# Two layers of a hybrid decoder on one core: a transpose moved to another PSUM bank and the layer norm's first steps issued ahead of the head norms

## The reference

```python
h = _rmsnorm(x, mix_norm_g[l])
a_b, a_c, a_x, s_u, s_v, q, k, v, gates = _split_cols(h @ w_in[l])
ya = _short_conv(a_b, a_c, a_x, conv_w[l], conv_b[l])
# spatial gating: v goes through gelu, a layer norm, then a causal 128x128 mixing
v = _layernorm(jax.nn.gelu(s_v), ln_g, ln_b);  yb = gelu(s_u) * (tril(w_s) @ v + b)
# stick-breaking attention, 8 heads x 64
qh = _rmsnorm(q.reshape(B, S, 8, 64), q_norm_g[l]); kh = _rmsnorm(k..., k_norm_g[l])
yc = _stick_breaking(qh, kh, vh)
x = x + (sum_i sigmoid(gate_i) * (y_i @ w_branch_out[i])) @ w_o[l]
x = x + SwiGLU(_rmsnorm(x, ffn_norm_g[l]))
```

## Time and profile before

| | us |
|---|---|
| three runs, median (lowest to highest) | 1691.32 (1690.37 to 1693.25) |
| profiled execution, its own time | 1691.32 |
| its span from first to last instruction | 1689.6 |
| PE busy / DVE / ACT / POOL | 1673.9 / 970.6 / 738.0 / 220.3 |

### The profile page before, as it was taken

The page is one execution under the profiler, slowest core; times in us unless marked ns, Lnnn a source line. Parts: engine busy times, 40 slices in busy tenths (PEclk is TensorE's granted clock), DMA queues, the critical chain, the costliest instruction groups (busy, mean ns, idle before and its releaser), DMA issues.

```text
span 1689.6 us, 22191 instructions
## 1 busy us (share of the span) xinstructions
PE 1673.9 (99%) x7651; PEld 1392.9 (82%) x7651; DVE 970.6 (57%) x1180; ACT 738.0 (44%) x1033; POOL 220.3 (13%) x204
## 2 busy tenths in 40 slices
PE   8999999999999999999999999999999999999998
PEld 6888888888888888888878888888888888888887
DVE  6887876554555434434659877765555543444344
ACT  5677676433343223223346776763333432232232
POOL 3343221000130000000323233200002100000000
PEclk9999999999999999999999999999999999999999
DMA  6232323333333333333333222223333333333333
GB/s 173 81 97 75 99 63 90 91 92 95 106 96 92 99 100 98 90 98 99 116 109 100 75 87 87 87 69 99 94 99 100 93 94 100 99 95 93 99 99 112
DMA packets 307416, 162.19 MB, mean 96 GB/s; under 512 B 5424, under 2 KB 303528, under 8 KB 307368
## 3 DMA queue, kind: packets, MB, share of 16 engines
q1 hardware_dynamic: 305064, 157.37, 31.9%
q10 hardware_dynamic: 2304, 4.20, 0.7%
HBM read 155.25 MB, written 2.10 MB: 93 GB/s over the span
## 4 chain that ended last, share of the span: by engine, by line
PE 92%; DVE 3%; DVEq 2%; ACT 1%; POOLq 0%; issue 0%; POOL 0%; DMA 0%; ACTq 0%; SPq 0%
PE bank L525 28%; PE bank L529 28%; PE bank L526 28%; PE z L598 2%; PE z L529 1%; PE z L525 1%; PE z L526 1%; DVEq L1594 1%; PE z L571 1%; PE misc L614 1%; PE misc L612 1%; PE z L572 1%; DVE S L1323 0%; DMA gates<-in_x 0%; DVE w_lo L1192 0%
## 5 line engine op out<-in xcount | busy, mean ns | idle before, releaser
L525 PE MATMUL bank<-xg_hi,w_hi 128*128 128x512 f32 x1584 | 622.7, 393 | 2.1 <-DVE xg_lo L1599 2.1
L526 PE MATMUL bank<-xg_lo,w_hi 128*128 128x512 f32 x1584 | 617.7, 390 | 0.0
L836 ACT ACTIVATE w_hi<-raw 128x1024 fp32r<-128x1024 f32 (+1 forms) x296 | 305.5, 1035 | 550.0 <-DMA raw<-in_w_gate_up 223.6
L1192 DVE TENSOR_TENSOR w_lo<-raw,w_hi 128x1024 fp32r<-128x1024 f32 (+1 forms) x296 | 387.2, 1311 | 37.6 <-ACT w_hi L836 21.3
L529 PE MATMUL bank<-xg_hi,w_lo 128*128 128x512 f32 x1584 | 392.4, 389 | 0.0
L525 PEld LDWEIGHTS bank<-xg_hi,w_hi 128*128 128x128 f32 x1584 | 298.0, 188 | 64.3 <-DVE xg_lo L1599 2.5
L526 PEld LDWEIGHTS bank<-xg_lo,w_hi 128*128 128x128 f32 x1584 | 298.1, 188 | 61.4 <-issue 0.7
L529 PEld LDWEIGHTS bank<-xg_hi,w_lo 128*128 128x128 f32 x1584 | 297.3, 188 | 62.1 <-issue 0.5
L1197 DVE TENSOR_TENSOR S<-bank,rstd 128x512 f32<-128x512 f32 x152 | 104.9, 690 | 267.5 <-PE bank L529 266.9
L525 PE MATMUL bank<-mid_hi,w_hi 128*128 128x512 f32 x480 | 186.9, 389 | 0.0
L526 PE MATMUL bank<-mid_lo,w_hi 128*128 128x512 f32 x480 | 186.7, 389 | 0.0
(11 more groups left out here) (205 smaller groups left out, 1689.9 us busy)
## 6 DMA issues: line engine op xcount, KB each, us to landing
raw<-in_w_in SPq DMA_DIRECT2D x112, 512.0 KB, 3.7
raw<-in_w_gate_up SPq DMA_DIRECT2D x88, 512.0 KB, 3.8
raw<-in_w_down SPq DMA_DIRECT2D x48, 512.0 KB, 3.5
raw<-in_w_branch_out SPq DMA_DIRECT2D x16, 512.0 KB, 3.6
raw<-in_w_o SPq DMA_DIRECT2D x16, 512.0 KB, 3.5
raw<-in_w_branch_out SPq DMA_DIRECT2D x16, 256.0 KB, 2.6
gates<-in_x SPq DMA_DIRECT2D x4, 512.0 KB, 7.1
mix_hi<-yb_hi ACTq DMA_DIRECT2D x8, 256.0 KB, 2.3
```

The source lines that it names most:

```text
L525: mm(dst[:, :], wh[:, k0 + k, :], his[k], start=(k % per == 0), stop=False)
L526: mm(dst[:, :], wh[:, k0 + k, :], los[k], start=False, stop=False)
L836: af(w_hi[at.slot(c)][:, 0:kc, :], raw[at.slot(c)][:, 0:kc, :], ACT.Copy).then_inc(hi_done, 1)
L1192: tt(w[:, 0:kc, :], r[:, 0:kc, :], h[:, 0:kc, :].bitcast(F32), ALU.subtract).then_inc(lo_done, 1)
```

## The change

The fourth `v` block's transpose goes to the bank `misc` instead of `z[0]`, and stands alone between units 5 and 6. The Q squares' two matmuls go from behind unit 5 to behind unit 6, the K squares' from behind unit 6 to behind unit 7. `misc` is thus lent five times in the stage instead of four (`M_P`), and POOL's K squares wait for one count more of `misc_done`. On ACT the fourth `keep_tokens` and the layer norm's four tiny operations now stand ahead of both `rms_chain`s, and the K rounding stands behind the first `ln_round`. On DVE the statistics stand right behind `scaled(5)`, the inverse root's last steps ahead of both `head_norm`s, `layer_norm(0)` ahead of `q_rest`, and `head_norm` of K ahead of `layer_norm(1)`. Seven small tiles get other addresses; none of them shares its place with another in either version.

```diff
-M_P, M_PAIR, M_PAIR_LAST = 4, 6, 3
+M_P, M_PAIR, M_PAIR_LAST = 5, 6, 3
@@ tiles: eps, par, gain0 now behind sw_lo, conv_in behind KT
-        sv_bank = [z[0], z[2], z[1], z[0]]
+        sv_bank = [z[0], z[2], z[1]]
@@ gpsimd
-                head_square(l * 8 + 2, KT, m0 + 2)
+                head_square(l * 8 + 2, KT, m0 + 3)
@@ tensor
                 unit(at, 5, xh, xl)
-                head_squares(m0 + 1, l * 8 + 1)
-                pe.wait_ge(sv_ok, l * 4 + 4)
-                pe.wait_ge(sv_kept, l * 4 + 1)
-                turn(sv_bank[3], lambda n: gates[:, 3, n * P:(n + 1) * P]).then_inc(sv_turned, 1)
+                four_transposes(m0 + 1, lambda n: gates[:, 3, n * P:(n + 1) * P], sv_ok, l * 4 + 4)
                 unit(at, 6, xh, xl)
-                head_squares(m0 + 2, l * 8 + 2)
+                head_squares(m0 + 2, l * 8 + 1)
                 unit(at, 7, xh, xl)
+                head_squares(m0 + 3, l * 8 + 2)
                 unit(at, 8, xh, xl)
-                four_transposes(m0 + 3, lambda n: sw_raw[:, n, :], sw_masked, l + 1)
+                four_transposes(m0 + 4, lambda n: sw_raw[:, n, :], sw_masked, l + 1)
@@ scalar
                 split_hi(at, 8)
+                act.wait_ge(misc_done, m0 + 2)
+                keep_tokens(3, misc).then_inc(sv_kept, 1)
+                act.drain()
+                act.sem_inc(misc_free, 1)
                 ln_exp_table()
-                act.wait_ge(misc_done, m0 + 2)
-                rms_chain(nchain + 1, misc, HD, misc_free)
-                act.wait_ge(sv_turned, l * 4 + 4)
-                keep_tokens(3, sv_bank[3]).then_inc(sv_kept, 1)
-                split_hi(at, 9)
-                act.wait_ge(qk_nrm, l * 8 + 1)
-                q_round()
-                act.wait_ge(misc_done, m0 + 3)
-                rms_chain(nchain + 2, misc, HD, misc_free)
                 act.wait_ge(ln_var, l + 1)
                 ... (the layer norm's four tiny operations)
-                split_hi(at, 10)
+                act.wait_ge(misc_done, m0 + 3)
+                rms_chain(nchain + 1, misc, HD, misc_free)
+                split_hi(at, 9)
+                act.wait_ge(qk_nrm, l * 8 + 1)
+                q_round()
+                act.wait_ge(misc_done, m0 + 4)
+                rms_chain(nchain + 2, misc, HD, misc_free)
+                ln_round(l, 0)
                 act.wait_ge(qk_nrm, l * 8 + 2)
                 k_round()
-                ln_round(l, 0)
+                split_hi(at, 10)
                 ln_round(l, 1)
+                ln_round(l, 2)
                 split_hi(at, 11)
-                ln_round(l, 2)
@@ vector
                 scaled(at, 5, KT[:, :])
-                split_lo(at, 8)
-                head_norm(nchain + 1, QT, par[:, R_GQ:R_GQ + 1])
                 ... (bn_stats and bn_aggr of the four token blocks)
+                split_lo(at, 8)
                 scaled(at, 6, gates[:, 4, :])
-                q_rest(l * 8 + 1)
-                split_lo(at, 9)
-                head_norm(nchain + 2, KT, par[:, R_GK:R_GK + 1])
-                scaled(at, 7, gates[:, 5, :])
                 ... (the inverse root's last steps, ln_t and ln_rstd)
+                head_norm(nchain + 1, QT, par[:, R_GQ:R_GQ + 1])
+                split_lo(at, 9)
                 layer_norm(0)
+                q_rest(l * 8 + 1)
+                scaled(at, 7, gates[:, 5, :])
+                head_norm(nchain + 2, KT, par[:, R_GK:R_GK + 1])
                 layer_norm(1)
+                layer_norm_lo(0)
                 split_lo(at, 10)
-                layer_norm_lo(0)
                 layer_norm(2)
```

More of the change, by code:

```diff
@@ L149, in build @@
         sw_lo = sb("sw_lo", [P, KC, P], F32R)
+        eps = sb("eps", [P, 1])
+        par = sb("par", [P, 64])
+        gain0 = sb("gain0", [P, KD])
         ya_hi = sb("ya_hi", [P, KC, T], F32R)
@@ L174, in build @@
         KT = sb("KT", [P, T])
+        conv_in = sb("conv_in", [P, 2 + T])
         N0 = sb("N0", [P, T])
         N1 = sb("N1", [P, T])
+        N2 = conv_in[:, 2:2 + T]
+        sq_sum, sq_one = S2[:, :], N1[:, :]
         over = plan[0]
@@ L199, in build @@
         plan[0] = max(plan[0], over + 16 * 4 * T)
[L200 to L205, removed]
         assert plan[0] <= nc.sbuf_usable_end, plan[0]
@@ L967, in _ @@
                 for c in range(3):
-                    act.wait_ge(sv_turned, l * 4 + c + 1)
+                    act.wait_ge(sv_turned, l * 3 + c + 1)
                     keep_tokens(c, sv_bank[c]).then_inc(sv_kept, 1)
                 split_hi(at, 8)
+                act.wait_ge(misc_done, m0 + 2)
+                keep_tokens(3, misc).then_inc(sv_kept, 1)
+                act.drain()
+                act.sem_inc(misc_free, 1)
                 ln_exp_table()
-                act.wait_ge(misc_done, m0 + 2)
-                rms_chain(nchain + 1, misc, HD, misc_free)
-                act.wait_ge(sv_turned, l * 4 + 4)
-                keep_tokens(3, sv_bank[3]).then_inc(sv_kept, 1)
-                split_hi(at, 9)
-                act.wait_ge(qk_nrm, l * 8 + 1)
-                q_round()
-                act.wait_ge(misc_done, m0 + 3)
-                rms_chain(nchain + 2, misc, HD, misc_free)
                 act.wait_ge(ln_var, l + 1)
@@ L989, in _ @@
                 af(ln_t[:, :], ln_r[:, :], ACT.Square).then_inc(ln_chain, 1)
-                split_hi(at, 10)
+                act.wait_ge(misc_done, m0 + 3)
[6 more added lines that the diff above has]
+                ln_round(l, 0)
                 act.wait_ge(qk_nrm, l * 8 + 2)
                 k_round()
-                ln_round(l, 0)
+                split_hi(at, 10)
                 ln_round(l, 1)
+                ln_round(l, 2)
                 split_hi(at, 11)
-                ln_round(l, 2)
-                act.wait_ge(misc_done, m0 + 4)
+                act.wait_ge(misc_done, m0 + 5)
                 af(sw_hi[:, :, :], misc[:, :].rearrange("p (g t) -> p g t", g=KC), ACT.Copy).then_inc(sw_hi_ok, 1)
```

## The result

| | before | after |
|---|---|---|
| median of 4 runs, us | 1691.7 (1690.37 to 1693.25) | 1707.45 (1707.22 to 1708.33) |
| ratio to before | | 1.0094, 95% interval 1.0082 to 1.0107 |
| profiled execution / its span | 1691.32 / 1689.6 | 1705.47 / 1703.8 |

The kernel became 15.8 us slower. The forecast was 1697.2, with a range to 1699.4: the direction was right, the forecast rise of 5.9 us a little over a third of what came.

A forecast was written before the change was run, and what follows sets the result against it. The prediction took PE's own work to bound the kernel: 1691.3 + 4.2 (net waits at the first scores, 2.1 in each of two layers) + 1.7 (one half-clock stretch) = 1697.2 us, range 1692.6 to 1699.4.

The forecast's parts named there:

- The moved tile addresses: Small tiles at new addresses: no instruction's shape changes, so cost 0, with no bound known but the measurement's.
- PE's own list: PE's matmuls and transposes in stage P: same number of each, only reordered, so its own work changes by 0.
- The K path: Q squares to K rest, stage P: K rest starts at 73.4, PE waits 2.3 us at the first scores, net 2.1 per layer.
- case A: The forecast itself: `layer_norm_lo(0)` goes ahead of POOL's K rest, wait 2.3 us a layer, 1695.5 to 1698.9 us; chance 0.62.
- the 0.4 at the next pair's squares: PE's 0.21 us wait for the next pair's K squares: 0.2 us comes back per layer.
- Same busy sums: Second layer's stage P is the first's shifted by 834.4 us, so the net 2.1 us counts twice: 4.2 us.
- The K squares: POOL's K squares in stage P: done by 61.8, needed at 63.46, margin 1.6 us; the last holds DVE's Q norm up to 0.75.
- The clock: After PE's new waits at the scores: one 3.4 us stretch at half clock charged for the two, 1.7 us.
- C: First scores: `k_ok` comes in time, PE waits nothing, 1690.9 to 1691.5 us; chance 0.09.
- B: POOL goes first at the close call before the scores: wait 1.25 us, net 1.05 a layer, 1693.4 us; chance 0.20.
- D: More is late: K squares miss 63.46, or the wait grows to 3.0 with two slow stretches, 1700.3 us; chance 0.09.

The follow-up runs named there:

- e2: Kernel before with only the block of tile declarations changed, old order of all engines: 1702.64 us, ratio 1.0074.
- e3: Kernel before with only `mid_hi` and `mid_lo` moved 32 bytes further on: 1698.63 us, ratio 1.0051.
- e6: Kernel before with the `w_hi` weight tiles declared last, 32 bytes off the old alignment, and `eps` in a free column of `par`: 1718.25 us, ratio 1.0158.
- e9: Kernel before with streamed and weight tiles alike 32 bytes further on, and `eps` in a free column of `par`: 1691.47 us, ratio 0.9999.
- e1: Kernel before with the change's new order of the engines, every tile at its old address: 1696.23 us, ratio 1.0031.
- e7: New order at old addresses, plus DVE waiting before the first `layer_norm_lo` until POOL's K rest is done: 1696.82 us, against 1696.23 without that wait.
- e4: Kernel before with only `mid_hi` and `mid_lo` moved 64 bytes further on: 1694.09 us, ratio 1.0025.
- e13: Kernel before with only `mid_hi` and `mid_lo` moved 256 bytes further on: 1689.73 us in one run, beside 1690.01 of before.

## Why the forecast was wrong, step by step

- **"The moved tile addresses change no instruction's shape; I take 0 and know of no bound but that of the measurement."** This step failed: it held only that the instructions stay the same, and overlooked that the small tiles push the large ones behind them to other places. e2, which has only them, is 11.9 us slower; after's matmuls on `mid` step at 233.4 instead of 226.7 ns, e3 gets 233.3 with 32 bytes alone, and e6 with e9 show that the distance to the weight tile decides. "PE's own list: 0" counted instructions, and the count was right (7651 both times); their price had changed. A bound could have been had: the change moves the operands of 2016 matmuls, and 1% of their time, for instance, is 4.6 us.
- **The K path.** Right in each step, and a bit long at the end: the Q squares forecast at 57.56 and read at 57.34, the K rest at 73.4 and started at 73.08, its duration 4.0 and 3.96, the wait 2.3 and 1.96. The order on DVE and POOL was case A: `layer_norm_lo` first and unhindered (0.68), then the weight split held (1.89). e1 confirms it alone: 3.8 us of waits at the scores in both layers, with 4.6 forecast; the 0.4 at the next pair's squares went, as forecast, which leaves 3.4 against 4.2. Two readings in it were not exact. "Same busy sums" holds of PE only: DVE has 30.66 us in the first window and 28.36 in the second; the second layer's wait came out the same even so. And two unhindered K rest operations were put at 2.4 us, where e7 has 2.64.
- **The K squares** held the Q norm's first operation as forecast (1.34 instead of 0.69) and were in time.
- **The clock.** One stretch of 1.7 us was charged to the new waits. In the profiled execution of after neither was followed by one (the windows behind each):

```profile
77.20:80.60 3.40, 3.40 (x19) 3.00 (x20) 3.16 (x6) 2.06 (x3) 0.00 (x0) 1.00 0.43 126
917.70:921.10 3.40, 3.40 (x19) 3.01 (x20) 3.16 (x6) 2.06 (x3) 0.00 (x0) 1.00 0.40 120
```

  In e1 the second was, 1.3 us after PE went on (its wait ended at 914.75). The window there and the next, at the clock levels of 1.2 and 2.4 GHz:

```profile
916.10:919.50 3.40, 3.40 (x11) 2.82 (x11) 3.23 (x5) 2.59 (x5) 0.00 (x0) 0.50 0.01 2
919.50:922.90 3.40, 3.40 (x16) 2.79 (x16) 3.28 (x6) 3.37 (x6) 0.00 (x0) 1.00 0.00 0
```

  e9 and e4, without any new wait, had two stretches each near 31 and 857 us, e3 and e13 none. So they come and go by the execution. The charge of one was a guess that these traces neither bear out nor refute.
- **The rivals.** C is out (there is a wait). Of A, B and D only A's mechanism is seen, at 1.96 us. With the order alone the time is e1's 1696.2, inside the range and 1.0 from the forecast (a rise of 5.5 against 5.9). Part of that closeness is luck: the waits came out 0.8 us less than forecast, and the clock term was the guess above. No rival held the mechanism that made three quarters of the loss.

## What to carry to other kernels

A line that only declares a tile is part of a change's cost: where PE is the bound and streams from one tile while it loads weights from another, compare the addresses of both builds, and keep the distance between the two a multiple of 256 bytes, the only ones seen here at the full pace (pad small tiles, or declare them behind the large ones). When busy time grows at an equal count of instructions, read start-to-start steps of one long row before looking for a wait. And when a wait is removed by making another engine wait, look one step down the chain for where it comes out.

## What the runs showed of the hardware that I had not expected

- 128x512 matmuls with a weight load beside each step at 226.7 ns when streamed tile and weight tile lie a multiple of 256 bytes apart, at 229.0 at 64, and at 232.9 to 234.3 at the other multiples of 32; these are means, and single steps at one distance differ by up to 8 ns (229.1 and 237.5 at 128). Shifting both by 32 bytes changes nothing (0.9999). The weight loads themselves show 187 to 189 ns in every case.
- The mean step is the same to 0.1 ns in row after row of 192 matmuls, so one profile tells it where the total time needs many runs.
- A busy 99% hides it wholly: no wait, no clock change and no traffic differs between the two 43 us windows.
